# Two transformer blocks in one program: the first norm's opening work is dealt out anew between ScalarE, VectorE, GpSimd and TensorE

## What is computed

```
def _rmsnorm(x, g):
    xf = x.astype(jnp.float32)
    r = lax.rsqrt(jnp.mean(xf * xf, axis=-1, keepdims=True) + EPS)
    return (xf * r).astype(x.dtype) * g
...
def _mixer(x, mem, norm_mix_g, ...):
    h = _rmsnorm(x, norm_mix_g)
    proj = h @ w_in                     # 1024 x 9216: gates, convolutions, queries
    ...                                 # two convolution branches, attention to mem
    return merged @ w_o
...
first block:   x = x + _mixer(x, ...);  x = x + _conv_ffn(x, ...);  rmsnorm
second block:  two layers, each attention and a squared-ReLU MLP;    rmsnorm
```

## Time and profile before

| | us |
|---|---|
| median of 3 runs | 1150.17 |
| the runs | 1149.3, 1150.17, 1151.92 |
| the profiled execution, its own time | 1149.22 |
| its span in the trace | 1147.0 |
| TensorE busy | 1128.1 (98%) |
| VectorE, ScalarE, GpSimd busy | 828.1, 625.8, 480.8 |

### The profile page before, as it was taken

One profiled execution on the slowest core, in us unless ns is written; L12 is line 12 of the kernel. 1 busy time (PEld: TensorE's weight loads), 2 busy tenths in 40 slices (PEclk: granted clock), 3 DMA queues, 4 the chain that ended last, 5 costly groups with the idle time before them and its releaser, 6 DMA issues.

```text
span 1147.0 us, 18238 instructions
## 1 busy us (share of the span) xinstructions
PE 1128.1 (98%) x6858; PEld 996.7 (87%) x6858; DVE 828.1 (72%) x1070; ACT 625.8 (55%) x850; POOL 480.8 (42%) x405
## 2 busy tenths in 40 slices
PE   8999999999999999999999999999999999999997
PEld 8999999888998888888897788888888767888886
DVE  4778988987875898777897577566666666656655
ACT  7554443666634666555668755444464687444443
POOL 2799998898101633333223438880010345000000
PEclk9999999999999999999999999999999999999999
DMA  9655555563447456555542287556555514565550
GB/s 303 202 174 180 189 173 183 183 219 111 138 157 241 153 184 209 193 167 192 159 147 100 77 241 240 187 190 209 183 172 196 179 42 138 198 202 191 189 183 37
DMA packets 142807, 201.06 MB, mean 175 GB/s; under 512 B 3300, under 2 KB 123108, under 8 KB 142748
## 3 DMA queue, kind: packets, MB, share of 16 engines
q1 hardware_dynamic: 141776, 196.88, 52.2%
q0 software_dynamic: 912, 3.17, 1.2%
q10 hardware_dynamic: 60, 0.20, 0.1%
HBM read 199.20 MB, written 1.05 MB: 175 GB/s over the span
## 4 chain that ended last, share of the span: by engine, by line
PE 91%; issue 2%; POOL 2%; DVE 2%; ACT 2%; POOLq 0%; ACTq 0%; DVEq 0%
PE ps L1974 52%; PE ps L2011 22%; PE ps L2016 11%; PE ps L2222 1%; PE ps L2120 1%; PE ps L2182 1%; POOL wlo L484 1%; PE ps L2170 1%; PE ps L2102 1%; POOL merged L578 0%; PE ps L2269 0%; DVE p_parts L1199 0%; PE ps L2088 0%; ACT ps L727 0%; POOL p_parts L476 0%
## 5 line engine op out<-in xcount | busy, mean ns | idle before, releaser
L1172 DVE TENSOR_TENSOR wlo<-raw,whi 128x2048 fp32r<-128x2048 f32 (+1 forms) x162 | 376.9, 2327 | 131.4 <-ACT whi L643 130.7
L643 ACT ACTIVATE whi<-raw 128x2048 fp32r<-128x2048 f32 (+1 forms) x178 | 337.5, 1897 | 140.3 <-PE ps L1974 133.3
L2011 PE MATMUL ps<-p_parts,whi 128*128 128x512 f32 x1184 | 289.3, 390 | 0.0
L2011 PEld LDWEIGHTS ps<-p_parts,whi 128*128 128x128 f32 x1184 | 220.1, 188 | 44.7
L1974 PE MATMUL ps<-p_parts,whi 128*128 128x256 f32 x912 | 164.8, 283 | 0.6 <-DVE p_parts L1199 0.6
L2016 PE MATMUL ps<-p_parts,wlo 128*128 128x256 f32 x1184 | 163.3, 282 | 0.0
L2016 PEld LDWEIGHTS ps<-p_parts,wlo 128*128 128x128 f32 x1184 | 155.8, 191 | 5.5
L1974 PE MATMUL ps<-whi,q_hi 128*128 128x512 f32 x380 | 148.6, 391 | 0.2 <-POOL wlo L484 0.2
L1974 PE MATMUL ps<-whi,q_lo 128*128 128x512 f32 x380 | 148.3, 390 | 0.0
L1974 PE MATMUL ps<-wlo,q_hi 128*128 128x512 f32 x380 | 147.9, 389 | 0.0
L1974 PEld LDWEIGHTS ps<-p_parts,whi 128*128 128x128 f32 x912 | 142.4, 192 | 1.1 <-issue 1.0
(11 more groups left out here) (305 smaller groups left out, 1742.3 us busy)
## 6 DMA issues: line engine op xcount, KB each, us to landing
raw<-in_w_in SPq DMA_DIRECT2D x35, 1024.0 KB, 5.0
raw<-in_w_up SPq DMA_DIRECT2D x22, 1024.0 KB, 5.1
raw<-in_up_a SPq DMA_DIRECT2D x16, 1024.0 KB, 5.4
raw<-in_down_a SPq DMA_DIRECT2D x16, 1024.0 KB, 4.9
raw<-in_up_b SPq DMA_DIRECT2D x16, 1024.0 KB, 5.3
raw<-in_down_b SPq DMA_DIRECT2D x16, 1024.0 KB, 4.9
raw<-in_od_w_qkv SPq DMA_DIRECT2D x12, 1024.0 KB, 5.2
raw<-in_w_down SPq DMA_DIRECT2D x11, 1024.0 KB, 4.9
```

Of the source, the lines that this page charges most:

```text
L643: nc.scalar.activation(whi[:, g % R, 0:n], raw[:, g % R, 0:n], ACT.Copy).then_inc(hi_ready, 1)
L1172: nc.vector.tensor_tensor(wlo[:, g % R, 0:n], raw[:, g % R, 0:n], whi[:, g % R, 0:n].bitcast(F32), ALU.subtract).then_inc(lo_ready[g % R], 1)
L2011: return nc.tensor.matmul(bank(2 * pb + h), whi[:, r, at], p_parts[:, :, S * k:S * k + S], start=k == 0, stop=False)
```

## The change

GpSimd now waits for VectorE's piece of group 0 (`first_lo`) ahead of its own first piece, not ahead of its third. ScalarE squares both halves of `x`; VectorE copies the vectors and scales both halves of the rows, and multiplies the two rows of vectors later, between `lo(1)` and `lo(2)`. The parts of the transposed rows are made by turns of banks, and the first product takes its blocks in that order. The transposes of the identity (9, 9 and 1) become products of the identity with itself repeated, 256 columns each (3, 2 and 2).

```diff
@@ -527,12 +527,12 @@
                     lo_piece(*piece)
 
             inverse_root("n_mix")
+            pool.wait_ge(first_lo, 1)
             for n in range(1, 4):
                 if n < 3:
                     pool.wait_ge(first_hi, n + 1)
                 else:
                     pool.wait_ge(hi_ready, 1)
-                    pool.wait_ge(first_lo, 1)
                 part = slice(BW * n, BW * n + BW)
                 nc.gpsimd.tensor_tensor(out=wlo[:, 0, part], in0=raw[:, 0, part], in1=whi[:, 0, part].bitcast(F32),
                                         op=ALU.subtract).then_inc(lo_ready[0] if n == 3 else first_lo_pool, 1)
@@ -658,7 +658,7 @@
             def norm_upper(name, dst):
 
                 m, b0 = TNORMS.index(name), NORM_BANK.get(name, 0)
-                turns = name not in ("n_mix", "n_mem", "n_mix2a")
+                turns = name not in ("n_mem", "n_mix2a")
                 for c in BY_TURNS if turns else range(KD):
                     act.wait_ge(norm_tr, 4 * m + c // 2 + 1)
                     if turns and c % 2:
@@ -822,10 +822,8 @@
             act.dma_start(vec_rows, d["vecs"]).then_inc(vec_in, 16)
             act.wait_ge(x_in[0], 16)
             nc.scalar.activation(o_up[:, :], x[:, 0, :], ACT.Square, accum_out=sm[:, 0:1]).then_inc(norm_sq, 1)
-            act.wait_ge(vec_tr, 1)
-            nc.scalar.activation(vec[:, :], bank(0, 0, KD * NV), ACT.Copy).then_inc(bank_read[0], 1)
-            act.wait_ge(norm_r, 1)
-            nc.scalar.activation(xn[:, 0, :], x[:, 0, :], ACT.Copy, scale=rr[:, 0:1]).then_inc(first_rows, 1)
+            act.wait_ge(x_in[1], 16)
+            nc.scalar.activation(o_low[:, :], x[:, 1, :], ACT.Square, accum_out=sm[:, 1:2]).then_inc(norm_sq, 1)
             act.wait_ge(bank_read[0], 1)
             for n in range(4):
                 act.wait_ge(raw_in[0] if n == 3 else first_in[n], 16)
@@ -1346,13 +1344,10 @@
                 nc.vector.tensor_scalar(ms[:, t:t + 1], sm[:, t:t + 1], 1.0 / D, EPS, ALU.mult, ALU.add).then_inc(norm_ms, 1)
 
             first_mean_square(0)
-            dve.wait_ge(x_in[1], 16)
-            nc.vector.tensor_tensor_reduce(out=o_low[:, :], in0=x[:, 1, :], in1=x[:, 1, :], scale=1.0, scalar=0.0, op0=ALU.mult,
-                                           op1=ALU.add, accum_out=sm[:, 1:2]).then_inc(norm_sq, 1)
-            dve.wait_ge(bank_read[0], 1)
-            by_row = vec.rearrange("p (c n) -> p n c", n=NV)
-            nc.vector.tensor_tensor(by_row[:, V_FIN, :], by_row[:, V_FIN, :], by_row[:, V_MIX2, :],
-                                    ALU.mult).then_inc(vec_fin, 1)
+            dve.wait_ge(vec_tr, 1)
+            nc.vector.tensor_copy(vec[:, :], bank(0, 0, KD * NV)).then_inc(bank_read[0], 1)
+            dve.wait_ge(norm_r, 1)
+            nc.vector.tensor_scalar(xn[:, 0, :], x[:, 0, :], rr[:, 0:1], None, ALU.mult).then_inc(first_rows, 1)
             first_mean_square(1)
             dve.wait_ge(norm_r, 2)
             nc.vector.tensor_scalar(xn[:, 1, :], x[:, 1, :], rr[:, 1:2], None, ALU.mult).then_inc(norm_xn, 2)
@@ -1360,6 +1355,10 @@
             nc.vector.tensor_tensor(wlo[:, 0, 0:BW], raw[:, 0, 0:BW], whi[:, 0, 0:BW].bitcast(F32), ALU.subtract).then_inc(first_lo, 1)
             norm_lower("n_mix", p_hi, p_lo)
             lo(1)
+            dve.wait_ge(bank_read[0], 1)
+            by_row = vec.rearrange("p (c n) -> p n c", n=NV)
+            nc.vector.tensor_tensor(by_row[:, V_FIN, :], by_row[:, V_FIN, :], by_row[:, V_MIX2, :],
+                                    ALU.mult).then_inc(vec_fin, 1)
             lo(2)
 
 
@@ -1981,7 +1980,7 @@
                     pe.wait_ge(lo_ready[g % R], g // R + 1 + i)
                 r = g % R
                 for h in range(2):
-                    for k in range(KD):
+                    for k in BY_TURNS if after == "n_mix" else range(KD):
                         if after == "n_mix" and h == 0 and k % 2 == 0:
                             done, n = ((first_lo, 1), (first_lo_pool, 1), (first_lo_pool, 2), (lo_ready[0], 1))[k // 2]
                             pe.wait_ge(done, n)
@@ -2263,23 +2262,24 @@
 
             pe.wait_ge(const_ready, 2)
 
-            def turn_identity(count):
+            def identity_products(count):
 
                 for n in range(count):
-                    nc.tensor.transpose(bank(6, P * (n % 4), P * (n % 4) + P), ident[:, :], ident[:, :])
-
-            turn_identity(9)
+                    nc.tensor.matmul(bank(6, S * (n % 2), S * (n % 2) + S).rearrange("p (b n) -> p b n", b=2), ident[:, :],
+                                     ident[:, :].unsqueeze(1).to_broadcast([P, 2, P]), start=True, stop=True)
+
+            identity_products(3)
             pe.wait_ge(vec_in, 16)
             for c in range(KD):
                 last = nc.tensor.transpose(bank(0, NV * c, NV * (c + 1)), vec_rows[:, P * c:P * c + P],
                                            ident[0:NV, 0:NV])
             last.then_inc(vec_tr, 1)
-            turn_identity(9)
+            identity_products(2)
             pe.wait_ge(cwf_in, 16)
             for k in range(K_F):
                 last = nc.tensor.transpose(bank(5, FT * k, FT * (k + 1)), cwf_rows[:, P * k:P * k + P], ident[0:FT, 0:FT])
             last.then_inc(vec_tr, 1)
-            turn_identity(1)
+            identity_products(2)
             transpose_norm("n_mix")
             phases = (("ugq", G_UGQ), ("cvb", G_CVB))
```

## The result

The changed kernel took 1152.52 us in the median of 20 runs (1150.27 to 1152.83), the kernel before 1150.28 (1149.3 to 1152.32). The ratio is 1.0016, with a 95% interval of 1.0010 to 1.0022: slower by 0.16%, clear of noise and just inside what I had called no difference. The median itself lies 0.2 us above my range (1149.0 to 1152.3), which was set on a kernel before at 1150.17; the ratio on that 1150.17 gives 1152.0, inside it. The profiled execution took 1152.27 us with a span of 1150.1, so 3.05 us more than the one shown before, where I had worked out 0.81.

The account below looks back on a forecast made before the run. TensorE, busy 98% of the span, was taken as the bound. Row transposes 0.58 us later plus 0.23 for turns gave 0.81: 1150.0 on the profiled execution, 1151.0 on the median; forecast 1150.5 us, range 1149.0 to 1152.3.

Parts of the forecast that it names:

- 0.81: Summed delay of the first product in us: 0.58 from later row transposes plus 0.23 from turns of banks.
- The bound and the place: TensorE bounds the kernel; the change acts only through when the first product starts (13.33 us before) and its speed.
- Same: Verdict that the measured time shows no clear difference, between 1147.9 and 1152.5 us; chance 0.88.
- Two, with 0.05 us for the first after a change of operands, are 0.90 us: Price of the two identity products just before the row transposes, 0.63 us more than the one transpose they replace.
- cost nothing directly: The earlier three and two identity products (1.3 and 0.9 us) end before the landings that follow them.
- Rival A: Clock rises before the row transposes; first product at 12.98, 0.35 us sooner, 1148.9 us; chance 0.15.
- Rival B: Clock rises later, at 17.7 us; first products at half speed lose 1.6 us, 1151.6 or 1152.6 us; chance 0.15.
- Turns of banks: Between bank 0 whole and the first product, four steps stand in line: 2.08 us against 1.85, 0.23 more.
- a stall of up to 0.3: Possible wait in us ahead of group 1 of the first product, its 0.5 us cover just used up.
- The moved squares, copy and scaling: ScalarE and VectorE work in the opening: rows ready sooner, but TensorE comes later, so worth nothing.
- The wait of GpSimd: GpSimd's pieces ready at 14.6 us instead of 14.3; the first product wants the last at 15.9, so nothing.
- Nothing that the change edits lies behind that point: Behind the next transposes at 65.40 us the change edits nothing; any difference there would show the forecast wrong.

Follow-up runs that it names:

- e2: The kernel before with only the identity products of the change (3, 2 and 2) added: 1151.71 us.
- e4: The changed kernel with four identity products filling TensorE's idle stretch in the memory attention, ahead of the first product with values: 1150.78 us.
- e5: The changed kernel with the old identity transposes and block order 0 to 7, leaving only squares, copy, scaling and GpSimd's wait moved: 1149.4 us.
- e10: e9 with the small conv-weight transposes put behind the row transposes and the single identity transpose removed: 1148.82 us.
- e1: The changed kernel with the old identity transposes (9, 9 and 1) in place of the products: 1149.91 us.
- e11: The kernel before with only GpSimd's wait for VectorE's piece put ahead of its first piece: 1150.32 us.
- e12: The kernel before with only the squares, copy and scaling moved, GpSimd's wait left where it was: 1149.87 us.
- e6: The kernel before with four identity products filling TensorE's idle stretch in the memory attention: 1149.66 us.
- e9: e5 with the idle stretch of the memory attention filled by identity products: 1149.21 us.

## Why the prediction was off, step by step

**The bound and the place: right.** TensorE had to start its first product sooner or later, and everything behind moved with it. The direction was right, and the size was too small: 0.81 forecast, 3.05 between the two profiled executions, 2.2 between the medians. Of the 2.24 us between 0.81 and 3.05, 0.58 is the later first product (1.39 for 0.81), 0.16 the 432 matmuls, 1.37 a stretch that I had excluded, and 0.14 I cannot place. "Same" came out right all the same, which owes more to the width of that band, 2.3 us to either side, than to the sum.

**"Two, with 0.05 us for the first after a change of operands, are 0.90 us": the step that failed.** Measured, the four matmuls of the two products take from 9.46 to the row transposes' 11.25, 1.79 us. I had a float32 product priced by the 107 ns between a transpose and a matmul in the earlier trace rows. That row says x64; the code there (`pair_times_values`, 8 pairs, 2 by 2 products) has 32. It is two instructions for a product, and the count was in the row. The same mistake made the next sentence wrong: three and two products "cost nothing directly". They took 2.93 and 2.08 us, not 1.3 and 0.9, so the transposes of the vectors began at 5.96 and those of `cwf_rows` at 8.99, where the kernel before had them at 5.22 and 8.35. TensorE reached the rows 2.15 us later, not 0.58.

**Rival A's mechanism came true and did not pay.** The clock rose before the row transposes in the changed kernel's profile, and gave back 1.05 us of the 2.15 (ten transposes in 1.10 us); with 0.33 for the turns that makes 1.43, and 1.39 was measured. I had given it 0.15, and had left a mixture out: the price of the products and the earlier clock together. That is what the forecast should have priced. How early the clock rises differs from execution to execution: it had risen before 6.8 us in the profiles of e2 and e4, within the last products or the row transposes in others. In e4's profile rival A came true whole: ScalarE's pieces end at 11.17, the first product starts 2.08 us later, and the execution, whose idle stretch is filled, took 1149.25 where A had 1148.9. The Trainium skill's rule that transposes do not bring the clock up ("TensorE: Matmul & The Clock Gate", Part 4) is contradicted again: in e5, e10 and the kernel before, nothing but transposes ran before the first product, and its matmuls ran at the 2.4 GHz level from the first (432 in 52.07 us).

**Rival B, a later rise: not in any profile.** Every first product ran at the full level.

**Turns of banks: mechanism right, mis-sized.** 0.23 forecast; 0.33 measured (12.54 to 14.72 against 1.85; e1 against e5 the same), and the matmuls of the first phase take 0.14 to 0.19 us more (52.21 to 52.26 in the four profiles with turns, 52.06 or 52.07 in all others), for which I had given a stall of up to 0.3.

**The moved squares, copy and scaling: worth nothing for the start, as said, while TensorE is late** (e5, 13.32). The wait of GpSimd likewise: in e11 the first product starts at 13.33. What I did not foresee is that the moved work trims the slowest executions, and that it can matter once the clock rises early (e12).

**"Nothing that the change edits lies behind that point": true, and not enough.** 1.4 us came from the clock's fall after the idle stretch at 282 us. e4 shows that it is the clock, and e11 and e5 that it comes with the old opening too. The nearest rows were there before: TensorE stood still 2.47 us at 280.43 in the kernel before. I had looked for waits that the change moves, not for waits near which the granted clock may differ between two executions. Whether the changed opening also makes the fall more frequent is not settled: 17 of its 20 runs lay above 1151.7, but the runs' records do not separate a fall from a late opening. With the stretch filled in both kernels (e4 and e6), 1.1 us of the 2.2 between the medians are left, which would leave the other half to the stretch, as in the two profiles; but these are 12 and 11 runs that spread over 3 us, and their means differ by 0.5 only. The opening's share of the medians is therefore known roughly, and its cause, the products, well.

## What to carry to other kernels

Compare the count in a row with the number of calls in the code before taking its duration as the price of a call. Filler work put in front of a wait must end before what is waited for arrives, at the lower clock too; else it is on the path, and the clock it buys has to be worth more than that. And when single executions spread by more than the change, look for places where TensorE idles for microseconds: filling one (1.7 us of dead products) took 1.7 us off the changed kernel's median, and 0.5 and 0.2 off two others (e6, e9).

## What the runs showed of the hardware that I had not expected

- A float32 product of 256 columns of the identity went as two matmuls, each of 634 ns and 0.43 us after the other at the low clock; a float32 transpose of 128 columns went as one, 0.215 us after the other. Per column the product costs twice as much:

```profile
L2268 PE MATMUL ps<-ident x14: 511/634/795, 3.1 to 10.9; 128*128 128x256 f32 x14
```

- VectorE and GpSimd, subtracting at the same time, slowed each other; what they share was not tried apart. VectorE's subtraction of 128 by 512 took 1.77 us beside GpSimd's (the kernel before, e2, e12), and 0.68 or 0.69 alone. GpSimd's three pieces took 3.73 us alone and 4.23 beside it. e11 differs from the kernel before by the order of the two alone, and has 0.68 and 3.75. The changed kernel, timelines of VectorE and GpSimd:

```profile
9.92 0.68 DVE L1355 TENSOR_TENSOR wlo<-raw,whi 128x512 fp32r<-128x512 f32 x1
```
```profile
10.68 3.73 POOL L537 TENSOR_TENSOR wlo<-raw,whi 128x512 fp32r<-128x512 f32 x3 [1.54 <-DVE wlo L1355]
```

- One and the same opening started its first product at 13.25 and at 14.72 us, according to when the clock rose. And an idle stretch of 2.5 us was followed by 3.4 us at the 1.2 GHz level in seven of nine profiled executions; cut to 0.75 us, in none of five.
